# Two norm stages of a two-layer backbone: tokens turned by a diagonal matrix of inverse roots, modulation applied in the copies out of PSUM

## Chip, cores and metric

The program runs on one core of one Trainium2 chip, everything in float32. The metric is the device time of one launch in microseconds (us). Three runs of the kernel before gave 1813.14, 1815.0 and 1820.26 us, median 1815.0.

## What is computed

The reference has two layers over 256 latent and 256 context tokens of 1024 channels. Every layer starts with a modulated RMS norm of both streams, followed by a mixer whose first step is one large product:

```python
def rmsnorm(x, g):
    xf = x.astype(F32)
    y = xf * lax.rsqrt(jnp.mean(xf * xf, axis=-1, keepdims=True) + EPS)
    return (y * g.astype(F32)).astype(x.dtype)

def modulate(x, g, shift, scale):
    return rmsnorm(x, g) * (1.0 + scale) + shift

for layer in range(DEPTH):
    h_lat = modulate(x_lat, norm1_g[layer], mod_l[:, 0], mod_l[:, 1])
    h_ctx = modulate(x_ctx, norm1_g[layer], mod_c[0], mod_c[1])
    # layer 0: mixer_ab: h @ ab_w_in, latent attention, RG-LRU, output product
    # layer 1: mixer_cd: h @ cd_w_in, windowed attention, SSD, output product
    # then a second modulate and a mixture of experts on both streams (layer 1: latents only)
```

Shift and scale are rows of a product of the conditioning vector with `ada_w`; the kernel keeps them in a DRAM tensor `mod`, with (1 + scale) * g already folded together in the scale rows.

## The kernel before

The program is a chain of stages. Each stage is one `nc.Block()` with a program for each of the five engines (SyncE, ScalarE, VectorE, GpSimd, TensorE), and a block ends only when all five have finished theirs, so stages follow each other in time. Only DMAs that a stage issues without waiting for them reach over its end.

The tokens lie in SBUF as `x[128 tokens, 4 tiles, 1024]`; tiles 0 and 1 are the latent stream, 2 and 3 the context stream. The products that follow want the channels on the partitions: `ht[128, 8, 512]`, in which partition p of block k is channel 8p + k. `norm_stage` makes `ht` from `x`. It is called four times: for half 0 (ahead of the mixer) and half 1 (ahead of the experts) of both layers. It works in this order:

- SyncE (line 314) loads scale and shift rows of each stream, copied to all 128 partitions: 1 MB per stream. Behind them, by `prefetch` (line 358, `load_chunk`), it issues the first three chunks of the next product's weights into `ring[1]`: for layer 0 of 2, 1.5 and 2 MB, for layer 1 of 64 KB, 2 and 2 MB.
- ScalarE (line 321) squares the four tiles with a running sum per token; VectorE (334) makes means, ScalarE (323) roots, VectorE (336) reciprocals.
- VectorE, tile by tile: `h = x * root * scale` (line 340), then `h = h + shift` (line 342), 128x1024 each.
- TensorE (line 352): eight 128x128 transposes of each tile, against the identity, into two of the banks 0 to 3.
- ScalarE (line 328): two 128x512 copies of each tile from PSUM into `ht`.

After it comes `project_lru_stage` in layer 0 (products at line 541, the first 32 of them with 512 moving columns) and `project_ssd_stage` in layer 1 (line 1571; its first 32 products have only 16 moving columns, as they make the 16 step sizes of each token). The products of layer 0 start with chunk 0 of the weights, and take chunk 1 after four groups of eight.

Of the kernel before, what the change touches and what calls it, by code (L numbers as in the profile page):

```python
# [20 lines left out]
ALU = mybir.AluOpType  # L21
ACT = mybir.ActivationFunctionType
AX = mybir.AxisListType

P = 128
D = 1024
KC = D // P
SEQ = 256
NT = 4
LT = SEQ // P  # L30
T = NT * P
NMOD = 6
EPS = 1e-6
# [18 lines left out]
class Chain:  # L52
# [6 lines left out]
    def step(self, ins):  # L59
        self.n += 1  # L60
        ins.then_inc(self.sem, 1)
        self.engine.wait_ge(self.sem, self.n)
# [9 lines left out]
def cut(region, offset, *dims):  # L72

    n = int(np.prod(dims))
    flat = region[:, offset:offset + n]
    if len(dims) == 1:
        return flat
    names = "abcd"[:len(dims)]
    spec = f"p ({' '.join(names)}) -> p {' '.join(names)}"
    return flat.rearrange(spec, **{k: v for k, v in zip(names[1:], dims[1:])})  # L80
# [214 lines left out]
def mod_row(c, stream, layer, slot, n=1):  # L295

    at = (layer * NMOD + slot) * D
    return c.mod[stream, at:at + n * D].partition_broadcast(P)


def norm_stage(c, layer, half, tiles, prefetch=None, at=0):

    nc = c.nc
    streams = sorted({t // LT for t in tiles})
    gs = [cut(c.scr, at + s * 2 * D, 2, D) for s in range(2)]
    ss = c.stat[:, 0:NT]
    n = len(tiles)
    mod_in, sums, mean, root, h_ready, turned, ht_ready = (
        c.sem(x) for x in ("mod_in", "square_sums", "mean_ready", "root_ready", "h_ready", "h_turned", "ht_ready"))
    with nc.Block() as block:  # L310
        @block.sync
        def _(sp):
            for s in streams:
                sp.dma_start(gs[s].rearrange("p a b -> p (a b)"), mod_row(c, s, layer, 3 * half, 2)).then_inc(mod_in, 16)
            if prefetch:
                prefetch(sp)

        @block.scalar
        def _(act):
            for t in tiles:  # L320
                nc.scalar.activation(c.h[:, t, :], c.x[:, t, :], ACT.Square, accum_out=ss[:, t:t + 1]).then_inc(sums, 1)  # L321
            act.wait_ge(mean, 1)
            nc.scalar.activation(ss[:, 0:n], ss[:, 0:n], ACT.Sqrt).then_inc(root, 1)
            for t in tiles:
                act.wait_ge(turned, t + 1)
                for q in range(2):
                    b = 2 * (t % 2) + q
                    last = nc.scalar.activation(c.ht[:, 4 * q:4 * q + 4, t * P:(t + 1) * P], c.bank(b, 4, P), ACT.Copy)
                    last.then_inc(ht_ready, 1)

        @block.vector
        def _(dve):
            dve.wait_ge(sums, n)
            nc.vector.tensor_scalar(ss[:, 0:n], ss[:, 0:n], 1.0 / D, EPS, ALU.mult, ALU.add).then_inc(mean, 1)
            dve.wait_ge(root, 1)
            c.dve_chain.step(nc.vector.reciprocal(ss[:, 0:n], ss[:, 0:n]))
            dve.wait_ge(mod_in, 16 * len(streams))
            for t in tiles:
                g = gs[t // LT]
                c.dve_chain.step(nc.vector.scalar_tensor_tensor(c.h[:, t, :], c.x[:, t, :], ss[:, t:t + 1], g[:, 1, :],  # L340
                                                                ALU.mult, ALU.mult))
                nc.vector.tensor_tensor(c.h[:, t, :], c.h[:, t, :], g[:, 0, :], ALU.add).then_inc(h_ready, 1)  # L342

        @block.tensor
        def _(pe):
            for t in tiles:
                pe.wait_ge(h_ready, t + 1)
                if t >= 2:
                    pe.wait_ge(ht_ready, 2 * (t - 1))
                for k in range(KC):  # L350
                    b = 2 * (t % 2) + k // 4
                    last = nc.tensor.transpose(c.bank(b, 4, P)[:, k % 4, :], c.h[:, t, k::KC], c.ident[:])  # L352
                last.then_inc(turned, 1)


def load_chunk(c, sp, w_dram, w_in, chunk_of, ch):
# [869 lines left out]
def load_gate_up(c, m, sp, e, j):  # L1226
    load_matrix(c, m, sp, e, j, "moe_w_gate")
    load_matrix(c, m, sp, e, j, "moe_w_up")


def load_expert(c, m, sp, e, j):
    load_gate_up(c, m, sp, e, j)
    load_matrix(c, m, sp, e, j, "moe_w_down")


def load_router(c, m, sp):
    sp.dma_start(m.rw, c.i["router_w"].rearrange("(p k) e -> p k e", k=KC)).then_inc(m.small_in, 16)
    sp.dma_start(m.rb, c.i["router_b"].partition_broadcast(P)).then_inc(m.small_in, 16)
    sp.dma_start(m.count, c.i["count"]).then_inc(m.small_in, 16)
    sp.dma_start(m.before, c.i["before"].rearrange("p (a b) -> p a b", a=2)).then_inc(m.small_in, 16)  # L1240
# [189 lines left out]
def moe(c, m, tiles, out=None):  # L1430

    def ahead(sp):
        load_router(c, m, sp)
        load_expert(c, m, sp, 1, 1)

    norm_stage(c, m.layer, 1, tiles, ahead, at=15360 - 4 * D)
    route_stage(c, m, m.layer, tiles, lambda sp: load_gate_up(c, m, sp, 2, 2))
    experts_stage(c, m)
    combine_stage(c, m, m.layer, tiles, out)
# [406 lines left out]
def program(nc, ins, outs):  # L1846
    with ExitStack() as ctx:
# [14 lines left out]
        def first_chunks(sp):  # L1862
            for ch in range(3):
                load_chunk(c, sp, ins["ab_w_in"], w_in, CHUNKS_AB, ch)

        norm_stage(c, 0, 0, everyone, first_chunks)
        project_lru_stage(c, m, w_in)
        mla_stage(c, m, late)
# [5 lines left out]
        def clear_spare_blocks(pool):  # L1874
# [4 lines left out]
            for r in parts:  # L1879
# [6 lines left out]
                        QK ** -0.5, m.attn_t, m.p, m.pt, QK, sp_work=loads, md=last)  # L1886
        output_stage(c, 0, everyone, m.wo, (m.attn_t, m.gr), 11168, lambda sp: load_expert(c, mo, sp, 0, 0), clear_spare_blocks)
        moe(c, mo, everyone)
        c.clear_semaphores()

# [4 lines left out]
        def first_chunks(sp):  # L1895
            for ch in range(3):
                load_chunk(c, sp, ins["cd_w_in"], w_in, CHUNKS_CD, ch)

        norm_stage(c, 1, 0, everyone, first_chunks)
        project_ssd_stage(c, m, w_in)  # L1900
        wo_in = c.sem("cd_wo_in")

        def loads(sp):
# [8 lines left out]
                        HD ** -0.5, m.attn_t, m.p, m.pt, HD, sink=m.sink, mask=lambda t: (1 - t, m.far[:, t, :]))  # L1912
        output_stage(c, 1, range(LT), m.wo, (m.attn_t, m.y_t), 0)
        moe(c, mo, range(LT), outs["out"])


# [45 lines left out]
```

## Time and profile before

| | before |
|---|---|
| median of 3 runs | 1815.0 us |
| the profiled execution, its own time | 1814.77 us |
| its span, first to last instruction | 1813.0 us |
| mean granted TensorE clock | 0.851 |
| busy: TensorE, VectorE, ScalarE | 1316.5, 567.6, 395.9 us |
| norm stage of layer 0, half 0: first square to last copy | 40.34 to 60.12 us |
| norm stage of layer 1, half 0: first square to last copy | 986.90 to 1007.38 us |

Of the profile the reader needs three views. The timeline gives, for one engine, start, length and count of merged instructions, and in square brackets how long the engine was idle before them and who released it. The table of stretches gives busy time, granted TensorE clock (1.00 is 2.4 GHz, 0.50 is 1.2 GHz) and DMA share between two points of time. The view of one line gives the least, median and greatest duration of its instructions. PE is TensorE, DVE is VectorE, ACT is ScalarE, POOL is GpSimd, SP is SyncE.

### The profile page before, as it was taken

To read this page: it belongs to the slowest core of one execution; us is meant where nothing else is said; L and a number is where in the kernel's file an instruction comes from. 1 tells how busy PE (TensorE), PEld (TensorE's weight loads), DVE (VectorE), ACT (ScalarE), POOL (GpSimd) and SP (SyncE) were. 2 spreads that over 40 slices of the span, in tenths; PEclk is the share of its full clock that TensorE was granted. 3 is DMA by queue.
4 is the path that set the end of the run, shared out by engine and by line. 5 is a ranking of instruction groups with operands and counts; after the bars stand their busy time and mean duration, and the time that the engine had idled before them with its cause. 6 is when DMAs were issued, how large, how long until landed. Compare 5 with 4: busy or idle time off the path is not lost. (4 is left out here: it accounts for less than half of the span.)

```text
span 1813.0 us, 35116 instructions
## 1 busy us (share of the span) xinstructions
PE 1316.5 (73%) x14404; PEld 774.9 (43%) x14405; DVE 567.6 (31%) x1511; ACT 395.9 (22%) x867; POOL 39.3 (2%) x81
## 2 busy tenths in 40 slices
PE   3897979895767897667990998949766555576572
PEld 2455646544433454333660646725343222243241
DVE  0537555413311222111224435567231000011012
ACT  1243224202111232111221222235112111122120
POOL 0002010100000000000001000000000000000000
PEclk8898999995888899788995798959978777798796
DMA  7422987256699999999925310050289999999995
GB/s 267 155 76 79 330 294 287 90 210 285 252 430 428 429 429 429 429 429 429 429 103 194 136 66 4 1 232 1 88 368 430 430 428 429 430 428 428 429 429 221
DMA packets 82533, 519.35 MB, mean 286 GB/s; under 512 B 12045, under 2 KB 16370, under 8 KB 57002
## 3 DMA queue, kind: packets, MB, share of 16 engines
q1 hardware_dynamic: 73632, 494.03, 66.2%
q10 hardware_dynamic: 5146, 13.78, 2.0%
q0 software_dynamic: 3696, 10.73, 1.6%
q8 instruction: 40, 0.66, 0.1%
q14 instruction: 19, 0.16, 0.0%
HBM read 501.50 MB, written 17.01 MB: 286 GB/s over the span
## 5 line engine op out<-in xcount | busy, mean ns | idle before, releaser
L1305 PE MATMUL bank<-sb_ring,sb_scratch 128*32 128x256 f32 x3968 | 275.4, 439 | 149.7 <-DMA sb_ring<-in_moe_w_up 136.5
L1305 PEld LDWEIGHTS bank<-sb_ring,sb_scratch 128*32 128x32 f32 x3968 | 144.9, 126 | 277.4 <-issue 220.2
L1384 DVE TENSOR_TENSOR sb_scratch<-sb_scratch,bank 128x128 f32<-128x128 f32 x88 | 25.3, 287 | 742.1 <-ACT sb_scratch L1337 742.1
L1305 PE MATMUL bank<-sb_scratch 128*32 128x256 f32 x1664 | 125.6, 468 | 95.1 <-DMA sb_scratch<-in_moe_w_up 92.7
L1341 ACT ACTIVATE sb_ht<-bank 32x256 f32<-32x256 f32 x352 | 132.3, 376 | 274.8 <-PE bank L1315 271.8
L1293 PE MATMUL bank<-sb_h,sb_scratch 128*32 128x256 f32 x2256 | 140.7, 384 | 13.8 <-DVE sb_scratch L1371 13.8
L1305 PEld LDWEIGHTS bank<-sb_scratch 128*32 128x32 f32 x1664 | 63.3, 134 | 156.3 <-issue 137.0
L1315 PE MATMUL bank<-sb_ring,sb_scratch 128*32 128x256 f32 x1984 | 119.2, 380 | 9.8 <-issue 9.4
L1337 ACT ACTIVATE sb_scratch<-bank 128x128 f32<-128x128 f32 x88 | 24.4, 278 | 464.2 <-PE bank L1305 464.1
L1293 PEld LDWEIGHTS bank<-sb_h,sb_scratch 128*32 128x32 f32 x2256 | 74.1, 111 | 63.0 <-DVE sb_scratch L1371 14.1
L1315 PEld LDWEIGHTS bank<-sb_ring,sb_scratch 128*32 128x32 f32 x1984 | 67.5, 110 | 54.8 <-issue 20.5
L352 PE MATMUL bank<-sb_ident,sb_h 128*128 128x128 f32 x112 | 25.7, 402 | 82.7 <-DVE sb_h L342 82.7
L1571 PE MATMUL bank<-sb_ring,sb_ht 128*128 128x16 f32 (+2 forms) x192 | 60.7, 474 | 5.8 <-DVEq L1734 4.4
L352 PEld LDWEIGHTS bank<-sb_ident,sb_h 128*128 128x128 f32 x112 | 20.6, 215 | 88.7 <-DVE sb_h L342 88.7
L541 PE MATMUL bank<-sb_ht,sb_ring 128*128 128x512 f32 x128 | 57.0, 607 | 1.4 <-PEq L310 1.4
L1571 PE MATMUL bank<-sb_ht,sb_ring 128*128 128x512 f32 x128 | 57.2, 607 | 0.0
L1315 PE MATMUL bank<-sb_scratch 128*32 128x256 f32 x832 | 49.9, 380 | 4.1 <-issue 3.8
L1376 DVE STREAM_TRANSPOSE sb_scratch<-bank 128x256 f32<-128x256 f32 x90 | 38.9, 432 | 38.6 <-PE bank L1293 38.6
L1571 PEld LDWEIGHTS bank<-sb_ring,sb_ht 128*128 128x128 f32 x192 | 38.8, 242 | 24.4 <-issue 17.5
L321 ACT ACTIVATE sb_h<-sb_x 128x1024 f32<-128x1024 f32 x14 | 14.6, 1044 | 158.3 <-PEq L1024 89.8
L195 PE MATMUL bank<-sb_ring 128*32 128x128 f32 x1280 | 39.1, 277 | 8.2 <-DMA sb_ring<-in_ada_w 8.2
L1044 PE MATMUL bank<-sb_ring,sb_scratch 128*128 128x512 f32 x96 | 43.2, 592 | 0.0
(299 smaller groups left out, 1550.5 us busy)
## 6 DMA issues: line engine op xcount, KB each, us to landing
sb_ring<-in_moe_w_gate SPq DMA_DIRECT2D x44, 2048.0 KB, 28.4
sb_ring<-in_moe_w_up SPq DMA_DIRECT2D x44, 2048.0 KB, 32.9
sb_ring<-in_moe_w_down SPq DMA_DIRECT2D x44, 2048.0 KB, 35.5
sb_ring<-in_ada_w SPq DMA_DIRECT2D x20, 2048.0 KB, 14.5
sb_scratch<-in_moe_w_gate SPq DMA_DIRECT2D x20, 2048.0 KB, 32.9
sb_scratch<-in_moe_w_up SPq DMA_DIRECT2D x20, 2048.0 KB, 37.6
sb_scratch<-in_moe_w_down SPq DMA_DIRECT2D x20, 2048.0 KB, 39.9
sorted_out<-sb_ht ACTq DMA_DIRECT2D x88, 128.0 KB, 6.0
```

The lines of the kernel that those rows point to most:

```text
L195: last = self.c.nc.tensor.matmul(self.c.ps[bank][32 * q:32 * q + 32, 0:P], self.condk[:, k, :], w[:, k, q * P:(q + 1) * P], start=k == 0, ...
L352: last = nc.tensor.transpose(c.bank(b, 4, P)[:, k % 4, :], c.h[:, t, k::KC], c.ident[:])
L541: last = nc.tensor.matmul(c.ps[u % NB][:, 0:rhs.shape[1]], lhs, rhs, start=k == 0, stop=k == KC - 1)
L1044: last = nc.tensor.matmul(c.ps[u % 4][:], src, wo[:, k, q * BANK:(q + 1) * BANK], start=k == 0, stop=k == KC - 1)
L1293: last = nc.tensor.matmul(c.ps[0][MB * q:MB * q + MB, 0:DQ], m.pick[:, t, :], c.h[:, t, q * DQ:(q + 1) * DQ], start=t == 0, stop=t == nt - 1)
L1305: last = nc.tensor.matmul(c.bank(1, 2, FQ)[MB * q:MB * q + MB, :, :], m.xt[:, k, :], m.gu[j][:, :, k, q * FQ:(q + 1) * FQ], start=k == 0, ...
L1315: last = nc.tensor.matmul(c.ps[3][MB * q:MB * q + MB, 0:DQ], m.hmt[:, k, :], m.down[j][:, k, q * DQ:(q + 1) * DQ], start=k == 0, stop=k == ...
L1337: nc.scalar.activation(m.sg, c.ps[1][:, 0:FQ], ACT.Silu).then_inc(silu_r, 1)
L1341: last = nc.scalar.activation(m.yb[j][:, q * DQ:(q + 1) * DQ], c.ps[3][MB * q:MB * q + MB, 0:DQ], ACT.Copy)
L1376: v.transpose(m.xt, c.bank(0, MB, KC).rearrange("p j k -> p k j")).then_inc(xt_ready, 1)
L1384: v.tensor_tensor(m.hm, m.sg, c.ps[1][:, FQ:2 * FQ], ALU.mult).then_inc(hm_ready, 1)
L1571: last = nc.tensor.matmul(c.ps[bank_of(u)][:, 0:rhs.shape[1]], lhs, rhs, start=k == 0, stop=k == KC - 1)
```

## The change

`norm_stage` as it was is now called `norm_rows_stage` and still serves half 1 of both layers. Half 0 of both layers (ahead of the mixers) gets a new `norm_stage`:

- The 2 MB of broadcast rows are replaced by two loads of shift and scale as columns (`modcol`, each partition its own 8 shifts and 8 scales: two pieces of 32 bytes per partition and stream).
- The squares carry the factor 1/1024 themselves, and epsilon is the bias of the root. Means, roots and reciprocals are made per stream, so those of the latents don't wait for the context tiles.
- VectorE multiplies the identity by the tile's inverse roots: a 128x128 diagonal matrix (`diag`) for each tile.
- TensorE multiplies `x` with that diagonal, by `matmul` rather than `transpose`: eight 128x128 products a tile, into banks 4 to 7, two tiles of one stream side by side. The result is turned and normed at once.
- The copies out of PSUM, 128x256 each, apply scale and shift, which are now numbers per partition: banks 4 and 6 by ScalarE, 5 and 7 by VectorE.

```diff
-def norm_stage(c, layer, half, tiles, prefetch=None, at=0):
+def norm_rows_stage(c, layer, half, tiles, prefetch=None, at=0):
...
+def norm_stage(c, layer, half, tiles, prefetch=None, at=0):
...
+        @block.sync
+            for s in streams:
+                sp.dma_start(modcol[:, s], c.mod[s, row:row + 2 * D].rearrange("(a p k) -> p a k", a=2, k=KC)).then_inc(cols_in, 16)
...
+        @block.scalar
+            for s in streams:
+                for t in range(s * LT, (s + 1) * LT):
+                    nc.scalar.activation(c.h[:, t, :], c.x[:, t, :], ACT.Square, scale=D ** -0.5, accum_out=ss[:, t:t + 1]).then_inc(means, 1)
...
+                nc.scalar.activation(of_stream, of_stream, ACT.Sqrt, bias=eps).then_inc(roots, 1)
+            act.wait_ge(cols_in, 16 * len(streams))
+            for s in streams:
+                for b in (0, 2):
+                    act.wait_ge(turned, 4 * s + b + 1)
+                    for k in (2 * b, 2 * b + 1):
+                        last = nc.scalar.activation(c.ht[:, k, s * W:(s + 1) * W], c.bank(4 + b, 2, W)[:, k % 2, :], ACT.Identity,
+                                                    bias=modcol[:, s, 0, k:k + 1], scale=modcol[:, s, 1, k:k + 1])
...
+        @block.vector
+            for s in streams:
+                dve.wait_ge(roots, s + 1)
+                step(v.reciprocal(of_stream, of_stream))
+                for t in range(s * LT, (s + 1) * LT):
+                    v.tensor_scalar(diag[:, t, :], c.ident[:], ss[:, t:t + 1], None, ALU.mult).then_inc(scaled, 1)
+            dve.wait_ge(cols_in, 16 * len(streams))
+            for s in streams:
+                for b in (1, 3):
+                    dve.wait_ge(turned, 4 * s + b + 1)
+                    for k in (2 * b, 2 * b + 1):
+                        last = v.tensor_scalar(c.ht[:, k, s * W:(s + 1) * W], c.bank(4 + b, 2, W)[:, k % 2, :],
+                                               modcol[:, s, 1, k:k + 1], modcol[:, s, 0, k:k + 1], ALU.mult, ALU.add)
...
+        @block.tensor
+            for s in streams:
+                for b in range(4):
+                    if s > 0:
+                        pe.wait_ge((act_evicted, dve_evicted)[b % 2], 2 * (s - 1) + b // 2 + 1)
+                    for t in range(s * LT, (s + 1) * LT):
+                        pe.wait_ge(scaled, t + 1)
+                        for k in (2 * b, 2 * b + 1):
+                            last = nc.tensor.matmul(c.bank(4 + b, 2, LT, P)[:, k % 2, t % LT, :], c.x[:, t, k::KC], diag[:, t, :],
+                                                    start=True, stop=True)
+                    last.then_inc(turned, 1)
...
-    norm_stage(c, m.layer, 1, tiles, ahead, at=15360 - 4 * D)
+    norm_rows_stage(c, m.layer, 1, tiles, ahead, at=15360 - 4 * D)
```

What VectorE has in a row in layer 0 between the barrier at the start of the norm stage and its end, before (a name in square brackets is the semaphore waited for; `mod_in` is the broadcast rows, `dve_chain` VectorE's own last result):

```order
L334 TENSOR_SCALAR sb_stat<-sb_stat 128x4 [waits square_sums_29]
L336 RECIPROCAL sb_stat<-sb_stat 128x4 [waits root_ready_31]
L340 SCALAR_TENSOR_TENSOR sb_h<-sb_x,sb_stat,sb_scratch 128x1024 [waits mod_in_28,dve_chain_2]
L342 TENSOR_TENSOR sb_h<-sb_h,sb_scratch 128x1024 [waits dve_chain_2]
L340 SCALAR_TENSOR_TENSOR sb_h<-sb_x,sb_stat,sb_scratch 128x1024
L342 TENSOR_TENSOR sb_h<-sb_h,sb_scratch 128x1024 [waits dve_chain_2]
```

And with the change (`x_turned` is TensorE's finished bank):

```order
L403 RECIPROCAL sb_stat<-sb_stat 128x2 [waits roots_ready_31]
L405 TENSOR_SCALAR sb_scratch<-sb_ident,sb_stat 128x128 [waits dve_chain_2]
L405 TENSOR_SCALAR sb_scratch<-sb_ident,sb_stat 128x128
L403 RECIPROCAL sb_stat<-sb_stat 128x2 [waits roots_ready_31]
L405 TENSOR_SCALAR sb_scratch<-sb_ident,sb_stat 128x128 [waits dve_chain_2]
L405 TENSOR_SCALAR sb_scratch<-sb_ident,sb_stat 128x128
L411 TENSOR_SCALAR sb_ht<-bank,sb_scratch 128x256 [waits x_turned_33,mod_columns_in_28]
L411 TENSOR_SCALAR sb_ht<-bank,sb_scratch 128x256
```

The eight passes over 1024 columns are gone; four 128x128 passes and eight 128x256 copies stand in their place, and both reciprocals and all four diagonals come ahead of the first copy.

ScalarE in the same place, with the change:

```order
L381 ACTIVATE sb_h,sb_stat<-sb_x 128x1024 x2
L386 ACT_TABLE_LOAD [waits square_means_30]
L386 ACTIVATE sb_stat<-sb_stat 128x2 [waits eps_set_29]
L381 ACTIVATE sb_h,sb_stat<-sb_x 128x1024 x2
L386 ACTIVATE sb_stat<-sb_stat 128x2 [waits square_means_30]
L392 ACTIVATE sb_ht<-bank,sb_scratch 128x256 [waits x_turned_33,mod_columns_in_28]
L392 ACTIVATE sb_ht<-bank,sb_scratch 128x256
```

The root of the first stream has moved ahead of the last two squares, and there is one table load, as before.

TensorE in the same place, before and then with the change:

```order
L352 MATMUL bank<-sb_ident,sb_h 128x128 [waits h_ready_32]
L352 MATMUL bank<-sb_ident,sb_h 128x128 x7
L352 MATMUL bank<-sb_ident,sb_h 128x128 [waits ht_ready_34,h_ready_32]
L310 UNCONDITIONAL_BRANCH
L541 MATMUL bank<-sb_ht,sb_ring 128x512 [waits ab_w_in0_25]
```

```order
L424 MATMUL bank<-sb_scratch,sb_x 128x128 [waits roots_spread_32]
L424 MATMUL bank<-sb_scratch,sb_x 128x128
L424 MATMUL bank<-sb_scratch,sb_x 128x128 [waits roots_spread_32,ht_even_34]
L424 MATMUL bank<-sb_scratch,sb_x 128x128 [waits roots_spread_32,ht_odd_35]
L368 UNCONDITIONAL_BRANCH
L614 MATMUL bank<-sb_ht,sb_ring 128x512 [waits ab_w_in0_25]
```

There are 32 instructions before and 32 after, but they wait for a diagonal in place of a finished tile of `h`, and in the second stream for the bank to be copied out.

## Rows read from the trace of the kernel before

**Rows 1.** Timeline of layer 0's norm stage, ScalarE (start us, length us, instruction, [idle before])

```profile
40.34 1.06 ACT L321 ACTIVATE sb_h<-sb_x 128x1024 f32<-128x1024 f32 x1 [37.29 <-PEq L244]
42.35 0.19 ACT L321 ACTIVATION_READ_ACCUMULATOR sb_h<-sb_x 128x1 f32 x1
...
44.63 1.28 ACT L323 ACT_TABLE_LOAD   x1
45.92 0.21 ACT L323 ACTIVATE sb_stat<-sb_stat 128x4 f32<-128x4 f32 x1
...
59.03 1.09 ACT L328 ACTIVATE sb_ht<-bank 128x512 f32<-128x512 f32 x2 [0.59 <-PE bank L352]
```

**Rows 2.** The same stage, VectorE

```profile
46.16 0.18 DVE L336 RECIPROCAL sb_stat<-sb_stat 128x4 f32<-128x4 f32 x1 [1.35 <-ACT sb_stat L323]
47.88 1.28 DVE L340 SCALAR_TENSOR_TENSOR sb_h<-sb_x,sb_stat,sb_scratch 128x1024 f32<-128x1024 f32 x1 [1.54 <-DMA sb_scratch<-mod]
49.20 1.22 DVE L342 TENSOR_TENSOR sb_h<-sb_h,sb_scratch 128x1024 f32<-128x1024 f32 x1
```

**Rows 3.** The same stage and the start of the next, TensorE

```profile
50.48 1.97 PE L352 MATMUL bank<-sb_ident,sb_h 128*128 128x128 f32 x8 [13.21 <-DVE sb_h L342]
...
57.84 1.16 PE L352 MATMUL bank<-sb_ident,sb_h 128*128 128x128 f32 x8 [0.52 <-DVE sb_h L342]
```

**Rows 4.** Timeline of layer 1's norm stage: ScalarE's first and last, TensorE's first and next stage

```profile
986.90 1.06 ACT L321 ACTIVATE sb_h<-sb_x 128x1024 f32<-128x1024 f32 x1 [31.18 <-PEq L124]
1006.29 1.09 ACT L328 ACTIVATE sb_ht<-bank 128x512 f32<-128x512 f32 x2 [1.31 <-PE bank L352]
...
996.98 1.97 PE L352 MATMUL bank<-sb_ident,sb_h 128*128 128x128 f32 x8 [42.93 <-DVE sb_h L342]
1007.68 12.18 PE L1571 MATMUL bank<-sb_ring,sb_ht 128*128 128x16 f32 x64 [1.43 <-PEq L310]
```

**Rows 5.** Stretches, TensorE: length, busy (count), granted clock, DMA share, GB/s

```profile
57.00:57.50 0.50, 0.32 (x2) 0.84 1.03 381
60.50:61.00 0.50, 0.50 (x1) 0.57 1.04 381
63.50:64.00 0.50, 0.50 (x2) 0.52 0.55 125
64.00:64.50 0.50, 0.50 (x3) 1.00 0.27 63
1006.00:1007.00 1.00, 0.25 (x2) 0.97 0.00 0
1009.00:1010.00 1.00, 1.00 (x9) 0.74 0.11 12
1023.00:1024.00 1.00, 1.00 (x3) 0.94 1.04 408
```

**Rows 6.** Attention of layer 0, full clock, TensorE: transposes (L921) and plain products (L909)

```profile
L921 PE MATMUL bank<-sb_ident,sb_scratch x96: 270/273/331, 270.5 to 352.5; 128*128 128x128 f32 x96
L909 PE MATMUL bank<-sb_h,sb_ring x192: 272/273/323, 272.7 to 353.7; 128*64 128x128 f32 x192
278.10 1.09 PE L909 MATMUL bank<-sb_h,sb_ring 128*64 128x128 f32 x8
```

**Rows 7.** Layer 1 after the norm, VectorE: copies of two neighbouring groups of 16-column products

```profile
1016.49 0.17 DVE L1703 COPY sb_scratch<-bank 128x16 f32<-128x16 f32 x1 [3.24 <-PE bank L1571]
1019.90 0.17 DVE L1703 COPY sb_scratch<-bank 128x16 f32<-128x16 f32 x1 [3.24 <-PE bank L1571]
```

**Rows 8.** Views of single lines: duration ns, least/median/greatest

```profile
L1749 DVE TENSOR_SCALAR sb_ring<-bank,sb_scratch x44: 472/473/484, 1106.7 to 1179.4; 128x256 f32<-128x256 f32 x44
L785 ACT ACTIVATE sb_ring<-bank x8: 384/384/386, 219.0 to 243.4; 128x256 f32<-128x256 f32 x8
L1424 DVE TENSOR_SCALAR sb_scratch<-sb_scratch,sb_wsel x6: 745/746/931, 967.0 to 1805.3; 128x1024 f32<-128x1024 f32 x6
```

**Rows 9.** DMA issues and landings: chunks of ab_w_in (L358), then small loads (L515)

```profile
L358 SPq DMA_DIRECT2D sb_ring<-in_ab_w_in x3: 567/2969/4942, 41.2 to 44.8; - x3
DMA to landing us min/median/max: 12.0/15.6/17.9
...
L515 SPq DMA_DIRECT2D sb_scratch<-in_lru_w_a x4: 610/616/638, 62.2 to 65.5; - x4
DMA to landing us min/median/max: 2.2/2.3/2.4
```

More of the change, by code:

```diff
@@ L353, in _ @@
                 last.then_inc(turned, 1)
+def norm_stage(c, layer, half, tiles, prefetch=None, at=0):
+    nc = c.nc
+    streams = sorted({t // LT for t in tiles})
+    W = LT * P
+    ss, eps = c.stat[:, 0:NT], c.stat[:, NT:NT + 1]
+    diag = cut(c.scr, at, NT, P)
+    modcol = cut(c.scr, at + NT * P, 2, 2, KC)
+    cols_in, eps_set, means, roots, scaled, turned, act_evicted, dve_evicted = (
+        c.sem(x) for x in ("mod_columns_in", "eps_set", "square_means", "roots_ready", "roots_spread", "x_turned", "ht_even", "ht_odd"))
+    with nc.Block() as block:
+        @block.sync
+        def _(sp):
+            row = (layer * NMOD + 3 * half) * D
+            for s in streams:
+                sp.dma_start(modcol[:, s], c.mod[s, row:row + 2 * D].rearrange("(a p k) -> p a k", a=2, k=KC)).then_inc(cols_in, 16)
+            if prefetch:
+                prefetch(sp)
+        @block.scalar
+        def _(act):
+            for s in streams:
+                for t in range(s * LT, (s + 1) * LT):
+                    nc.scalar.activation(c.h[:, t, :], c.x[:, t, :], ACT.Square, scale=D ** -0.5, accum_out=ss[:, t:t + 1]).then_inc(means, 1)
+                if s == 0:
+                    act.wait_ge(eps_set, 1)
+                act.wait_ge(means, (s + 1) * LT)
+                of_stream = ss[:, s * LT:(s + 1) * LT]
+                nc.scalar.activation(of_stream, of_stream, ACT.Sqrt, bias=eps).then_inc(roots, 1)
[6 more added lines that the diff above has]
+                                                    bias=modcol[:, s, 0, k:k + 1], scale=modcol[:, s, 1, k:k + 1])
+                    last.then_inc(act_evicted, 1)
+        @block.vector
+        def _(dve):
+            step, v = c.dve_chain.step, nc.vector
+            v.memset(eps, EPS).then_inc(eps_set, 1)
+            for s in streams:
+                of_stream = ss[:, s * LT:(s + 1) * LT]
+                dve.wait_ge(roots, s + 1)
[9 more added lines that the diff above has]
+                                               modcol[:, s, 1, k:k + 1], modcol[:, s, 0, k:k + 1], ALU.mult, ALU.add)
+                    last.then_inc(dve_evicted, 1)
+        @block.tensor
+        def _(pe):
+            for s in streams:
[8 more added lines that the diff above has]
+                    last.then_inc(turned, 1)
```

## The prediction, on record before the changed kernel was run

> **What bounds the kernel now.** I read the timelines of the two norm stages first, then the table of stretches for TensorE's clock, then the views of single lines for prices. Stages follow each other behind barriers, so what counts is each changed stage's time from its first square to its last copy, and what the next stage finds when it starts.
>
> In layer 0 that time runs from 40.34 to 59.03 + 1.09 = 60.12, 19.8 us [rows 1]; in layer 1 from 986.90 to 1006.29 + 1.09 = 1007.38, 20.5 us [rows 4]. The end is set by a line of waits: four squares (4.3 us), table load and root (to 46.13), reciprocal, a wait of 1.54 us for the broadcast rows, and then four tiles of 1.28 + 1.22 us of VectorE [rows 1, 2]. TensorE starts only at 50.48, 10.1 us into the stage, and sits idle 0.5 us before every later tile, waiting for `h` [rows 3]. So VectorE bounds the stage, with the rows' landing ahead of it; TensorE's transposes are hidden but for the last tile.
>
> **The change, step by step, times from the stage's start.**
>
> *Up to the first product.* Two squares end at 42.35 + 0.19 = 42.54, that is 2.2 us; table load 1.28 and root 0.21 bring 3.7; reciprocal 0.18, 3.95 [rows 1, 2]. A 128x128 diagonal is not in the trace: 128x1024 of the same operation takes 0.75 [rows 8], a reciprocal of 4 columns 0.18, so it lies between 0.18 and 0.75; I take 0.2, nearest the small end. TensorE starts at **4.2** where it started at 10.1.
>
> *The products.* This is the term that grows. A transpose leaves one record in the trace, a plain float32 product two: attention has 96 products to be turned, and L921 has 96 records, while the products with the turned blocks are also 96 and L909 has 192 [rows 6]. So the 32 products make 64 records. One record with its weights costs at half clock 3.41 us / 16 = 0.213 [rows 7]; at full clock (1.09 - 0.27) / 7 = 0.117 [rows 6]. A product is then 0.43 or 0.23 us. I take 0.22 for the latter, since moving 128 columns at 2.4 GHz should take no more than half of 0.43.
>
> The clock decides the sum. The transposes began at 50.48 and the clock rose at about 57.1, 6.6 us later, with TensorE idle in between; the dense 512-column products began at 60.43 and the clock, which fell at 60.57, was back at 64.0, 3.5 us later [rows 3, 5]. The new products follow each other without a gap, so I take a rise 5 us after their start, with bounds of 3.4 and 6.7. Five us at half clock are 5 / 0.43 = 11.7 products; the other 20.3 take 4.5; together **9.5** (bounds 8.7 and 10.3).
>
> Nothing else is behind this. Stream 1's roots: squares to about 6.0, root, reciprocal and diagonals to 6.9, while TensorE is busy with stream 0 until past 10. A bank of four products takes 0.9 us or more; its two copies take 0.77 on ScalarE (384 each) and 0.95 on VectorE (473 each) [rows 8], and the engines alternate, so each has two banks' time for one. The columns: two small loads at the head of the queue. Small loads of 256 pieces landed in 2.3 us [rows 9]; first needed at 4.2 + 1.7 = 5.9. VectorE's copies stand behind both diagonals of stream 1, at 6.9, when its first bank is done at 7.6.
>
> *The tail.* Last product's length beyond the spacing and the semaphore 0.2, VectorE's last two copies 0.95. The stage takes 4.2 + 9.5 + 0.2 + 0.95 = **14.85 us**. Saved: 19.8 - 14.85 = **4.9** in layer 0, 20.5 - 14.85 = **5.6** in layer 1.
>
> *The next stage's weights.* The first chunk of layer 0 landed 12.0 after its issue at 41.2, so at 53.2 [rows 9], behind 2 MB of rows that are no longer loaded; the new stage ends at 40.34 + 14.85 = 55.2. It is there even unmoved. The second is needed four groups (over 27 us) later. In layer 1 the first chunk has 64 KB. No wait takes the place.
>
> *The clock in the next stage.* Before, the clock was high for only 3.4 us around the last transposes and fell just as layer 0's dense products started: 3.4 us at half clock, 1.7 lost [rows 5]. Now TensorE has been dense at full clock for over 4 us, and the pause is 0.95 + 0.2 + 0.3 (barrier) = 1.5 us, so I expect it to stay high: **1.7** saved. That stage ends on products and a VectorE chain that waits for them, so it passes on. In layer 1 the clock fell at 1009.5 in the 16-column products and stayed low until 1023 [rows 5]; it will fall there again, perhaps a little later: **0.4**.
>
> *Removed at no gain:* the 1.54 us wait for rows is within the 10.1 already counted; half 1's stages are unchanged.
>
> Sum: 4.9 + 5.6 + 1.7 + 0.4 = 12.6. The profiled execution took 1814.77 us, 0.2 under the median of 1815.0, so **1802.2 us**. With rises at 3.4 us: 5.7 + 6.4 + 1.7 + 1.5 = 15.3, 1799.5; at 6.7 us and no warm start: 4.1 + 4.8 = 8.9, 1805.9.
>
> **A rule beside the row.** The count of records says that a float32 product costs two transposes (0.43 against 0.21 us at half clock). The Trainium skill, page "TensorE: Matmul & The Clock Gate", section "Terms", says that transpose mode is four times faster for float32. By that rule a product would be 0.85 and 0.44 us, 5.9 products in the first 5 us and 26.1 x 0.44 = 11.5 after: 16.5 in place of 9.5, 7 us more in each stage, and a kernel of 1816. No row here shows a factor of four; this is rival D.
>
> **Rivals.**
>
> *B. The clock never rises inside the stage.* Then 32 x 0.43 = 13.7, the stage takes 19.0, and only 0.8 + 1.5 = 2.3 us are saved: **1812.5**, no change. For it: in layer 1 the clock stayed low from 996.98 to 1006 under transposes, 9 us [rows 4, 5]. Against: those had gaps, and gapless 512-column products raised it in 3.5 us.
>
> *C. The columns land late: the slower side.* The two loads are of 32-byte pieces, 512 in all, read from `mod`, ahead of 5.5 MB in one queue. After the banks of stream 0 are full (at about 10) TensorE stops. If the columns land at L, two copies (0.9), sixteen products at half clock (6.8) and the tail (1.15) follow: the stage takes L + 8.9, and breaks even at L = 11. At L = 17.9, as the last chunk [rows 9], it takes 26.8: 7.0 + 6.3 us lost, **1828**. Against: the 2.3 us of 256 pieces [rows 9]; each piece would have to cost many times as much.
>
> *D. A float32 product costs four transposes:* about **1816**, as worked out.
>
> *E. The saved time is partly given back* in the next stages: a fall of the clock in the 1.5 us pause, its return later than before, and banks waited for. About half of the gain: **1807.5**. For it: the clock fell at 60.57 after a stretch with a pause of the same length [rows 5]. Against: in that stretch TensorE was idle for well over half.
>
> **How the numbers follow.** The forecast has 0.78, B 0.08, C 0.03, D 0.03, E 0.08. The likeliest case's own range is 1799.5 to 1806. To leave out at most 2 in 10 I add E and a margin for sizes I took from other operations (diagonal, copies with two operands): **1798 to 1809**. A measurement of this kernel tells 0.5%, 9.1 us, from no change: the line is at 1805.9. Faster: nearly all of the forecast and a little of E, **0.79**. Same: B, most of E and D, **0.17**. Slower: C and a part of D, **0.04**.
>
> **What would show it.** In the new profile: the first product 4.2 us after the first square; 64 records at L424 in each stage, none with an idle time before it that matters; the clock rising once in the stage, 3.4 to 6.7 us after the first product; the last copy 14 to 15.7 us after the first square, by VectorE (L411); the first product at L614 at full clock. The forecast is wrong if TensorE waits for a copy or for the columns, if there are more than two records per product, or if the clock stays at 0.50 to the stage's end.

## The result: slightly slower, and the profile after

The changed kernel takes 1820.84 us (median of 22 runs, 1812.95 to 1828.7), the kernel before 1814.93 us in 22 runs beside it (1810.04 to 1822.27). The ratio is 1.0033, 95% interval 1.0022 to 1.0044: some 6 us slower, a small loss but clear of the noise, where 12.6 us faster was forecast. The profiled execution of the changed kernel took 1821.84 us, its span is 1820.0 us, the mean granted clock 0.850 as before (0.851).

Timeline of layer 0's norm stage in the changed kernel, ScalarE, VectorE and TensorE, against [rows 1 to 3]; lines of the new `norm_stage` are 358 to 426, and L614 is the first product of the next stage:

```profile
40.34 1.06 ACT L381 ACTIVATE sb_h<-sb_x 128x1024 f32<-128x1024 f32 x1 [37.23 <-PEq L244]
42.61 1.28 ACT L386 ACT_TABLE_LOAD   x1
58.44 1.02 ACT L392 ACTIVATE sb_ht<-bank,sb_scratch 128x256 f32<-128x256 f32 x2 [2.79 <-PE bank L424]
...
44.44 0.48 DVE L405 TENSOR_SCALAR sb_scratch<-sb_ident,sb_stat 128x128 f32<-128x128 f32 x2
60.35 0.99 DVE L411 TENSOR_SCALAR sb_ht<-bank,sb_scratch 128x256 f32<-128x256 f32 x2 [2.82 <-PE bank L424]
...
44.78 15.53 PE L424 MATMUL bank<-sb_scratch,sb_x 128*128 128x128 f32 x64 [7.55 <-DVE sb_scratch L405]
61.66 8.82 PE L614 MATMUL bank<-sb_ht,sb_ring 128*128 128x512 f32 x20 [1.35 <-PEq L368]
```

TensorE starts 4.4 us into the stage, near the forecast (4.2; it was 10.1 before), has 64 records, as forecast, and no idle time. But the 64 take 15.5 us, not 9.5. ScalarE and VectorE wait for TensorE's banks, up to 2.8 us each time. The stage ends at 61.34, 21.0 us after its start, against 19.8 before. Layer 1's is as long, where it had 20.5 before, against [rows 4]:

```profile
991.03 1.06 ACT L381 ACTIVATE sb_h<-sb_x 128x1024 f32<-128x1024 f32 x1 [31.17 <-PEq L124]
...
1011.04 0.99 DVE L411 TENSOR_SCALAR sb_ht<-bank,sb_scratch 128x256 f32<-128x256 f32 x2 [2.82 <-PE bank L424]
...
995.46 15.54 PE L424 MATMUL bank<-sb_scratch,sb_x 128*128 128x128 f32 x64 [37.27 <-DVE sb_scratch L405]
```

The clock did rise. The table of stretches for TensorE in layer 0's stage of the changed kernel (length, busy, count, granted clock, DMA share, GB/s; a count takes in what overlaps an edge):

```profile
45.00:49.00 4.00, 4.00 (x17) 0.50 1.05 396
51.00:55.00 4.00, 4.00 (x19) 1.00 1.06 380
```

Twice the clock, and almost the same number of records in four microseconds, 17 and 19. They are 0.240 us apart at 1.2 GHz and 0.238 at 2.4 GHz. So I looked at the loading of the stationary operand, which comes ahead of each record and is listed as PEld. The views of the two lines, changed kernel (both layers) and then the transposes of the kernel before in the stretch at full clock (57.8 to 59), against [rows 6]:

```profile
L424 PEld LDWEIGHTS bank<-sb_scratch,sb_x x128: 312/336/341, 44.8 to 1010.5; 128*128 128x128 f32 x128
```

```profile
L352 PEld LDWEIGHTS bank<-sb_ident,sb_h x8: 185/193/208, 57.8 to 58.6; 128*128 128x128 f32 x8
```

A load of `x[:, t, k::KC]` for a plain product takes 338 ns at half and 336 at full clock; the load of `h[:, t, k::KC]`, with the same step of eight elements, for a transpose takes 226 ns at half and 193 at full clock. The theory after this reading: the step in the stationary operand sets the pace of plain float32 products. The rival: a plain product with 128 moving columns costs 0.24 us a record in any layout. The second question is where the rest of the 6 us comes from, since the two stages, up to the next one's start, grew by only 1.2 and, over three executions of each kernel, 1.0 us on the mean.

### The profile page after: what moved, and what is told of

Same layout as the page of the kernel before. It is cut to its first block and busy times, and to the rows that moved or that the text cites. A ratio compares the mean times of both kernels' runs of the same rounds, so it can differ in the third digit from the quotient of the medians.

```text
span 1820.0 us, 35264 instructions
## 1 busy us (share of the span) xinstructions
PE 1335.8 (73%) x14468; PEld 798.6 (44%) x14469; DVE 558.2 (31%) x1521; ACT 395.6 (22%) x869; POOL 39.1 (2%) x81
## 5 line engine op out<-in xcount | busy, mean ns | idle before, releaser
L1366 PEld LDWEIGHTS bank<-sb_h,sb_scratch 128*32 128x32 f32 x2256 | 74.4, 111 | 62.7 <-DVE sb_scratch L1444 14.1
L1388 PEld LDWEIGHTS bank<-sb_ring,sb_scratch 128*32 128x32 f32 x1984 | 67.6, 110 | 54.7 <-issue 20.5
L424 PE MATMUL bank<-sb_scratch,sb_x 128*128 128x128 f32 x128 | 31.1, 416 | 44.8 <-DVE sb_scratch L405 44.8
L614 PE MATMUL bank<-sb_ht,sb_ring 128*128 128x512 f32 x128 | 55.3, 593 | 1.4 <-PEq L368 1.4
L424 PEld LDWEIGHTS bank<-sb_scratch,sb_x 128*128 128x128 f32 x128 | 30.7, 336 | 45.4 <-DVE sb_scratch L405 45.4
L195 PEld LDWEIGHTS bank<-sb_ring 128*32 128x32 f32 x1280 | 34.9, 112 | 14.5 <-DMA sb_ring<-in_ada_w 8.7
## 6 DMA issues: line engine op xcount, KB each, us to landing
sb_ring<-in_moe_w_down SPq DMA_DIRECT2D x44, 2048.0 KB, 35.9
sb_scratch<-in_moe_w_up SPq DMA_DIRECT2D x20, 2048.0 KB, 37.8
```

What stands on the lines that cost most here:

```text
L195: last = self.c.nc.tensor.matmul(self.c.ps[bank][32 * q:32 * q + 32, 0:P], self.condk[:, k, :], w[:, k, q * P:(q + 1) * P], start=k == 0, ...
L424: last = nc.tensor.matmul(c.bank(4 + b, 2, LT, P)[:, k % 2, t % LT, :], c.x[:, t, k::KC], diag[:, t, :], start=True, stop=True)
L614: last = nc.tensor.matmul(c.ps[u % NB][:, 0:rhs.shape[1]], lhs, rhs, start=k == 0, stop=k == KC - 1)
L1366: last = nc.tensor.matmul(c.ps[0][MB * q:MB * q + MB, 0:DQ], m.pick[:, t, :], c.h[:, t, q * DQ:(q + 1) * DQ], start=t == 0, stop=t == nt - 1)
L1388: last = nc.tensor.matmul(c.ps[3][MB * q:MB * q + MB, 0:DQ], m.hmt[:, k, :], m.down[j][:, k, q * DQ:(q + 1) * DQ], start=k == 0, stop=k == ...
```

## The experiments

**Layout (blocks_diag).** Channels in blocks of 128, so the stationary operand is contiguous; the weights' rows follow, and shift and scale come as rows that TensorE turns. Three of the edited places (`...` stands for lines left out):

```diff
-                            last = nc.tensor.matmul(c.bank(4 + b, 2, LT, P)[:, k % 2, t % LT, :], c.x[:, t, k::KC], diag[:, t, :],
+                            last = nc.tensor.matmul(c.bank(4 + b, 2, LT, P)[:, k % 2, t % LT, :], c.x[:, t, k * P:(k + 1) * P], diag[:, t, :],
...
-                 w_dram.rearrange("o (p k) n -> p (o k) n", k=KC)[:, :, c0:c0 + n]).then_inc(w_in[ch % 3], 16)
+                 w_dram.rearrange("o (k p) n -> p (o k) n", k=KC)[:, :, c0:c0 + n]).then_inc(w_in[ch % 3], 16)
...
-                sp.dma_start(modcol[:, s], c.mod[s, row:row + 2 * D].rearrange("(a p k) -> p a k", a=2, k=KC)).then_inc(cols_in, 16)
+                sp.dma_start(modrow[16 * s:16 * s + 16, :], c.mod[s, row:row + 2 * D].rearrange("(r p) -> r p", p=P)).then_inc(cols_in, 16)
...
+            nc.tensor.transpose(c.ps[0][:, 0:32], modrow, c.ident[0:32, 0:32]).then_inc(cols_t, 1)
```

> Channels kept in blocks of 128 (block k of ht is channels 128k to 128k+127, and the weights are loaded to match), so that the stationary operand of the diagonal products is contiguous, not every eighth element; shift and scale come as 32 rows of 128 and are turned by one small transpose. All else as in the change. Theory stride (the products are spaced by the loading of a stationary operand with a step of 32 bytes): records go from 0.24 us apart to 0.213 at half and about 0.11 at full clock, the 64 take 9 to 10 us in place of 15.5, each norm stage 14.5 to 15.5 us, and the kernel is some 12 us faster than the change, near 1808. Rival (a plain float32 product with 128 moving columns costs 0.24 us a record whatever the layout): 15.5 us as now, no change of time.

Measured: 1803.43 us (6 runs), kernel before 1817.49 in 11 runs on the same chip, ratio 0.9919 (0.9904 to 0.9934). Its timeline and the load's view in layer 0:

```profile
44.84 8.79 PE L430 MATMUL bank<-sb_scratch,sb_x 128*128 128x128 f32 x64 [2.13 <-DVE sb_scratch L409]
54.99 15.26 PE L620 MATMUL bank<-sb_ht,sb_ring 128*128 128x512 f32 x35 [1.35 <-PEq L370]
```

```profile
L430 PEld LDWEIGHTS bank<-sb_scratch,sb_x x64: 192/192/338, 44.8 to 53.2; 128*128 128x128 f32 x64
```

The same 64 records take 8.8 us. At full clock the load takes 192 ns and the records are 0.112 us apart (0.238 in the changed kernel); at half clock they are 0.213 apart (0.240). The stage, from its first instruction to the next stage's, takes 14.5 us in both layers; to the last copy in layer 0 it is 14.25, where the prediction had 14.85. The rival falls. The kernel gained 14.1 us on the kernel before, more than the 12.6 that the prediction had for the change, and came out lower than the 1808 expected of this run.

**How large a step (step_2, step_4).** As blocks_diag, with the channels in blocks of 256 or 512 that are read with a step of 2 or 4 elements:

```diff
-                            last = nc.tensor.matmul(c.bank(4 + b, 2, LT, P)[:, k % 2, t % LT, :], c.x[:, t, k * P:(k + 1) * P], diag[:, t, :],
+                            last = nc.tensor.matmul(c.bank(4 + b, 2, LT, P)[:, k % 2, t % LT, :], c.x[:, t, k // 2 * 256 + k % 2:(k // 2 + 1) * 256:2], diag[:, t, :],
```

> The diagonal products with a step of 2 elements (8 bytes) in the stationary operand (channels in blocks of 256, each read in two interleaved halves, weights and shift and scale to match). Contiguous gave 64 records in 8.8 us, a step of 8 gave 15.5. Theory rate (an element costs by the bytes that its step passes over): a small step costs nothing, 8.8 us. Theory packing (only contiguous elements are read two at a time or more): any step costs the same as 8, 15.5 us.

> The same with a step of 4 elements (16 bytes). Theory rate: between, or still 8.8 us. Theory packing: 15.5 us.

Measured, layer 0, step 2 and then step 4 (timeline, a stretch at full clock, the load's view):

```profile
44.79 10.57 PE L432 MATMUL bank<-sb_scratch,sb_x 128*128 128x128 f32 x64 [2.27 <-DVE sb_scratch L409]
...
51.00:55.00 4.00, 4.00 (x36) 1.00 1.06 386
...
L432 PEld LDWEIGHTS bank<-sb_scratch,sb_x x64: 196/197/331, 44.8 to 55.0; 128*128 128x128 f32 x64
```

```profile
43.26 15.20 PE L432 MATMUL bank<-sb_scratch,sb_x 128*128 128x128 f32 x64 [1.94 <-DVE sb_scratch L409]
...
50.00:54.00 4.00, 4.00 (x19) 1.00 1.06 383
...
L432 PEld LDWEIGHTS bank<-sb_scratch,sb_x x64: 309/329/332, 43.3 to 57.9; 128*128 128x128 f32 x64
```

In layer 1 they took 9.76 and 15.20 us. The 10.6 and 9.8 us of step 2 are more than the 8.8 of the contiguous layout, but most of that is the clock: in layer 0 it rose 6.2 us after the first product, in blocks_diag 2.9. At the same clock the records lie so (distance of one record from the next, us):

| step in elements (bytes) | at half clock | at full clock | load at full clock, ns |
|---|---|---|---|
| 1 (4), blocks_diag | 0.213 | 0.112 | 192 |
| 2 (8), step_2 | 0.213 | 0.118 | 197 |
| 4 (16), step_4 | 0.233 | 0.233 | 329 |
| 8 (32), changed kernel | 0.240 | 0.238 | 336 |

A step of 8 bytes costs next to nothing, 16 bytes cost nearly all that 32 do. Neither theory had that shape: it is a jump between 8 and 16 bytes, not a slope, and not any step at all. At half clock the step costs little, since the contiguous records are 0.213 us apart there too; what it takes away is the gain of the full clock. The totals of these single runs were 1811.6 and 1818.59 us, with 1816.43 for one run of the kernel before on the same chip.

**Transposes in place of products (scaled_turn).** VectorE multiplies by the inverse root, TensorE transposes as before, the rest as in the change:

```diff
-                    v.tensor_scalar(diag[:, t, :], c.ident[:], ss[:, t:t + 1], None, ALU.mult).then_inc(scaled, 1)
+                    v.tensor_scalar(c.h[:, t, :], c.x[:, t, :], ss[:, t:t + 1], None, ALU.mult).then_inc(scaled, 1)
...
-                            last = nc.tensor.matmul(c.bank(4 + b, 2, LT, P)[:, k % 2, t % LT, :], c.x[:, t, k::KC], diag[:, t, :],
-                                                    start=True, stop=True)
+                            last = nc.tensor.transpose(c.bank(4 + b, 2, LT, P)[:, k % 2, t % LT, :], c.h[:, t, k::KC], c.ident[:])
```

> VectorE multiplies x by the inverse root (one pass of 128x1024 a tile, 0.75 us) into h, and TensorE transposes h as before the change, one record a block; copies with scale and shift per partition as in the change. If the transposes with the same step cost 0.213 us at half clock and 0.11 to 0.13 at full (as the old ones did) the products' 15.5 us become 6 to 7, each norm stage 12 to 13.5 us in place of 21.0, the kernel 14 to 17 us faster than the change and 8 to 11 faster than before, near 1805. If the step costs a transpose as much as a product in this arrangement, 32 records at 0.24 take 7.7 us and the stage 14.

Measured: 1800.85 us (6 runs, 1792.93 to 1801.87), ratio to the kernel before 0.9893 (0.9872 to 0.9914). The timeline of layer 0, then of layer 1:

```profile
45.41 6.40 PE L424 MATMUL bank<-sb_ident,sb_h 128*128 128x128 f32 x32 [7.98 <-DVE sb_h L405]
...
986.04 5.59 PE L424 MATMUL bank<-sb_ident,sb_h 128*128 128x128 f32 x32 [37.77 <-DVE sb_h L405]
```

Stages of 12.6 and 11.8 us against 20.0 and 20.7. Its median is the lowest of all here, below both kernels; it is 2.6 us under blocks_diag, whose 6 runs (1802.13 to 1807.84) don't overlap with it. It keeps what was good in the change (roots per stream, scale and shift in the copies, no broadcast rows) and leaves out the diagonal. The expected total was 1805, and 12 to 13.5 us were expected for each stage.

**Which layer costs the time (layer0_only, layer1_only).** The new stage in one layer, `norm_rows_stage` in the other:

```diff
-        norm_stage(c, 1, 0, everyone, first_chunks)
+        norm_rows_stage(c, 1, 0, everyone, first_chunks)
```

> The change in layer 0's norm stage alone; layer 1's is as before. Theory direct (the time is lost in the changed stage and the one after it): stage +1.2 us, next stage -1.7 to 0, so -0.5 to +1.2 us against before. Theory knock-on (what the change does to the time at which later stages begin, against the changes of the clock, costs more than the stages themselves): layer 0's attention takes 91.8 or more in place of 89.9, and the kernel is 2 to 4 us slower than before.

> The change in layer 1's norm stage alone. Theory direct: norm stage and the product stage behind it together +1.2 us, so +1.2 us. Theory knock-on: attention of layer 1 takes 56.5 in place of 54.4 besides, so +3 us, and layer 0's attention is as before at 89.9.

Measured, 12 runs each, with 23 of the kernel before on the same chip (median 1818.12): layer 0 alone 1816.76, ratio 0.9990 (0.9977 to 1.0003); layer 1 alone 1822.95, ratio 1.0020 (0.9999 to 1.0042). In layer 0 the gain of the warm start (106.4 us in place of 108.1 in the stage behind) pays for the longer stage, as theory direct had it for the total; knock-on's 2 to 4 us did not come, though layer 0's attention was 92.9 us in the profile. In layer 1 the median is 4.8 us up, more than stage and next stage account for. The interval touches no change, so this alone would not carry the point. And in the profile of layer1_only neither theory had the stages right: layer 0's attention took 92.4 us where 89.9 was expected, and layer 1's 58.6, where knock-on had 56.5.

**Profiles repeated (before_again, before_third, after_again, after_third).** Nothing is edited in these.

> A second profile of the kernel before, to see which stages differ from one execution to the next with nothing changed. Theory S (the extra time sits in fixed places that the change moved): every stage but the mixers' clock-dependent ones repeats within 0.3 us, and attention of layer 0 again takes near 89.9 us and its output stage 57.1. Theory N (noise of the clock, the extra 6 us is not from the change in this one execution): attention and output stages scatter by 2 to 4 us between executions of the same kernel, by how long the clock is at 0.50 in them.

> A second profile of the changed kernel. Both theories: 64 records at L424 in 15.5 us in each norm stage, stages of 21.0 us, since the records were 0.24 us apart at either clock. Theory S: attention of layer 0 and its output stage again near 93.7 and 59.3 us. Theory N: they scatter, and may be as short as before.

> A third profile of the kernel before. Theory systematic (the change in layer 1 costs some 4 us from that norm stage to the end of the attention): that stretch takes 286.6 to 290 us, as in the four profiles so far with the old stage in layer 1 (mean 287.8 without the pause). Theory chance: it is spread as with the new stage, 290 to 294.6.

> A third profile of the changed kernel. Theory systematic: the stretch takes 290 us or more (four profiles so far: 289.9 to 294.6, mean 291.8), attention 56.5 or more. Theory chance: it may be 286.6.

The kernel before repeated itself, as theory S had it; the changed kernel's attention and output product of layer 0 did not. From the norm stage of layer 1 to the end of its attention the stretch was 286.6 to 286.7 us in all three of one and 289.9 to 290.0 in all three of the other, as theory systematic had it; but it was also 290.0 in layer0_only, which has the old stage in layer 1. Lengths in us, each from the first instruction of a stage to the first of the next, read from the timelines; three executions of each kernel:

| stage | before | changed |
|---|---|---|
| layer 0 norm | 20.0, 20.2, 19.9 | 21.3, 21.3, 21.3 |
| layer 0 products after it | 108.1, 108.1, 108.1 | 106.4, 108.0, 106.4 |
| next (latent attention's inputs) | 96.2, 96.0, 96.3 | 94.6, 96.5, 95.5 |
| layer 0 attention | 89.9, 89.9, 90.0 | 93.7, 91.8, 90.7 |
| layer 0 output product | 57.1, 57.1, 57.1 | 59.3, 57.1, 58.8 |
| layer 1 norm | 20.7, 19.4, 20.8 | 21.3, 21.3, 21.3 |
| layer 1 products and SSD | 188.9, 190.5, 188.9 | 189.6, 189.7, 189.7 |
| layer 1 attention | 54.5, 54.5, 54.5 | 56.5, 56.5, 56.5 |
| span | 1813.0, 1812.7, 1812.2 | 1820.0, 1815.1, 1815.8 |

By the means, the norm stages add 1.2 and 1.0, the products after them take 1.2 off and add 0.3: +1.3 together. Attention adds 2.2 and 2.0 and the first output product 1.3, though none of their instructions is changed: +5.5. The other stages give 2.4 back, which leaves the 4.4 us between the mean spans. So most of the loss in these six executions lies in stages that the change doesn't touch.

That the change causes it is not shown by this, least of all in layer 0. layer1_only and pause_before (below) run the kernel before's own instructions up to layer 1, and in both layer 0's attention took 92.4 us and the output product 58.8, as long as in the changed kernel. Of the 14 executions that were profiled only the three of the kernel before had 89.9 to 90.0 in this attention; the others had 90.7 to 93.7. The start of the attention, of the kernel before and then of layer1_only:

```profile
264.64:268.80 4.16, 4.12 (x6) 0.59 0.65 217
```

```profile
262.66:273.40 10.74, 8.99 (x24) 0.68 0.60 199
```

TensorE was at half clock for 3.4 us of this attention before, and for 10.1 us in layer1_only: 6.9 at its start and the rest at its end.

Layer 1's attention shows what such a difference is made of. The stretches, TensorE, of the kernel before from the stage's start at 1218.99, and then of the changed kernel from its start at 1224.4:

```profile
1218.99:1231.00 12.01, 11.03 (x23) 0.50 0.35 149
1231.00:1236.00 5.00, 4.65 (x23) 0.97 0.00 0
```

```profile
1224.40:1236.40 12.00, 11.01 (x23) 0.50 0.33 139
1236.40:1241.40 5.00, 5.00 (x16) 0.50 0.01 2
1241.40:1245.00 3.60, 3.35 (x18) 0.99 0.00 0
```

Both start at half clock, on the same work. Before, the full clock is back after 12 us; in the changed kernel after 17, and the stage is 2.0 us longer. In layer1_only it took 22 us and the stage 58.6. Its stretches:

```profile
1236.00:1241.00 5.00, 5.00 (x16) 0.50 0.00 0
1241.00:1246.00 5.00, 5.00 (x17) 0.50 0.01 2
1246.00:1250.00 4.00, 3.89 (x18) 0.99 0.00 0
```

In the 5 us before the clock came back TensorE was busy throughout in each of the three, and in layer1_only for 10 us ahead of these as well. So the busy time of these stretches doesn't say why it came back when it did; the guess was that it has to do with when the stage begins.

**A pause ahead of attention (pause_before, pause_after).** To move that beginning, one idle copy on ScalarE at the end of the stage ahead:

```diff
                 act.sem_inc(copied, 1)
+            c.act_chain.step(nc.scalar.activation(c.scr[:, 3200:4500], c.scr[:, 3200:4500], ACT.Copy))
```

> The kernel before with one idle copy on ScalarE (about 1.3 us) at the end of the stage ahead of layer 1's attention, so that attention begins that much later against the clock's changes. Theory knock-on: attention takes 56.5 in place of 54.4 though none of its work is changed, so the kernel gains 3.3 us and not 1.3. Rival (attention's length has to do with what the change left in memory or in PSUM, not with when it starts): 54.4.

> The changed kernel with the same idle copy. Theory knock-on: attention of layer 1, 56.5 in both profiles of the changed kernel, now takes 54.4; the pause is paid back. Rival: 56.5.

Measured: theory knock-on missed both. pause_before took 54.5 us in attention and pause_after 56.6, which is what the rival had (totals of single runs 1819.89 and 1828.37). As a test it was weak: the stages ahead came out at other lengths in these two executions (SSD 190.2 and 192.2), so the pause, 1.5 us, did not move the beginning to where it was meant. What can be read from all 14 executions is the time from the clock's last fall before attention, inside the SSD stage, to attention's start, and how long the clock then stayed at half, from that fall to its return within attention:

| from fall to start, us | half clock, from fall to return, us | layer 1 attention, us | executions |
|---|---|---|---|
| 35.4, 35.5, 35.5, 35.7 | 47.8 | 54.5, 54.5, 54.5, 54.4 | before, before_again, before_third, scaled_turn |
| 35.9, 36.0 | 58.0 | 58.6, 58.6 | step_2, layer1_only |
| 36.3 | 54.6 | 56.7 | blocks_diag |
| 37.4, 37.5, 37.5, 37.5, 37.5 | 54.6 | 56.6, 56.5, 56.5, 56.5, 56.7 | pause_after, changed, after_again, after_third, layer0_only |
| 37.8, 39.0 | 51.2 | 54.8, 54.5 | step_4, pause_before |

The code of layer 1's norm stage does not decide the length: scaled_turn and step_4 have a new stage there and 54.4 and 54.8, layer0_only has the old one and 56.7. That also speaks against the rival, what the change left in memory. The executions fall into groups by the moment of the start, but not in a simple order: a start 0.2 us later (35.7, 35.9) went with 4.2 us more, one 0.3 us later (37.5, 37.8) with 1.7 us less. No run set the moment on purpose and hit it, so it is not shown as a cause; nor is it shown that the change moves it for the worse in most executions.

## Why the prediction was wrong, step by step

- **Start at 4.2 us:** right (4.4). A diagonal took 0.28 us against 0.2 assumed, the root with a bias 0.30 against 0.21. Nothing waited for the columns: their two loads landed in 1.7 to 1.9 us. Rival C is out.
- **64 records:** right: two for each plain float32 product.
- **What a record costs: the step that failed.** The prediction took 0.213 us a record at half clock and 0.11 at full, from products whose stationary operand is contiguous [rows 6, 7], and gave the stationary operand `x[:, t, k::KC]` with its step of eight elements no cost of its own. That the transposes read with the same step and were fast said nothing of plain products. The changed kernel's 64 records took 15.5 us and not 9.5, 0.24 each at both clocks. The full clock is where it went: the forecast had 20.3 products at 0.22 us there, at 0.476 they take 5.2 us more (an estimate from the 0.238 us between records). The rest of the term was sound: with the step taken out it measured 8.8, with the clock rising 2.9 us after the first product, which is earlier than the forecast's bound of 3.4 (step_2, with the rise at 6.2, took 10.6). Twice 6 us of the forecast gain were lost here.
- **Clock inside the stage:** rose 5.5 us after the first product in layer 0 and 3.7 in layer 1, forecast 5, and bought nothing, since the load did not get faster with it. Rival B had 13.7 us for the products, nearer than 9.5, and its total of 1812.5, but its condition, a clock that stays low, did not come. By rival D, the factor of four from the Trainium skill, page "TensorE: Matmul & The Clock Gate", section "Terms", 16.5 us were due. The measured 15.5 is near. A factor of about four is seen at full clock with the step of eight (0.476 us a product, 0.11 a transpose in scaled_turn), but not at half clock (0.48 against 0.213), and contiguous it is two: two records 0.112 us apart against one for a transpose. So the factor is not the cause.
- **The tail and the copies:** two copies 0.99 us on VectorE (0.95 forecast); ScalarE's with scale and bias 560 ns each, not the 384 of a plain copy [rows 8]. No copy held TensorE up.
- **Warm start of the next stage, 1.7 us:** right in layer 0: 106.4 against 108.1 in two of three executions. TensorE's pause between the stages was 1.35 us, and in these two the clock stayed at 2.4 GHz over it. In after_again it fell in that pause, at 59.7, and was back at 63.2: there the stage took 108.0, as rival E had it. Layer 1's 0.4 did not come: 189.7 against a mean of 189.4 before.
- **What had no term at all:** attention and output product, together 5.5 us in the profiled executions. The prediction carried saved time through unchanged stages as if their lengths were fixed, and they differ by up to 4 us between executions. Rival E had the clock in the next stages, but only as giving back a gain. (Half of the gain of 12.6 from 1814.8 is 1808.5, and not its 1807.5; nothing hangs on it.)

With the record at its true cost, the prediction's own sum would have been: stage 4.4 + 15.5 + 0.2 + 0.99 = 21.1, so 1.3 and 0.6 us lost, 1.7 won in layer 0: no change. The medians of 22 runs are 6 us apart. In the profiled executions what lies above the sum is in attention and output product, less 2.4 us that other stages gave back; whether the change causes it, and how, is open.

## What to carry to other kernels

Before a transpose is replaced by a float32 product that does arithmetic on the way, look at the step of its stationary operand: contiguous or 8 bytes apart a record took 0.11 to 0.12 us at full clock, 16 or 32 bytes apart 0.23 to 0.24 us, at either clock, and there are two for each product. Scaling ahead of a transpose cost one short VectorE pass (0.75 us for 128x1024) and was the faster way here. And stages that nobody edited came out 2 to 4 us longer or shorter, also with the same instructions ahead of them: compare several profiled executions stage by stage before a few tenths of a per cent are put down to the edited lines.

## What was not expected of the hardware

- Loading 128x128 float32 for a plain product: 192 ns contiguous, 197 with a step of 2 elements, 329 with 4, 336 with 8, at full clock; at half clock 329 to 338 in every layout. For a transpose with a step of 8: 193 ns at full clock. Why the transpose is spared is open.
- Records 0.24 us apart at both granted clocks, 0.50 and 1.00: a rise of the clock that changes nothing.
- An unchanged attention stage of 54.4 to 54.8, 56.5 to 56.7 or 58.6 us, by whether the clock came back 12 to 13, 17 to 18 or 22 us after its start, and the same value to 0.1 us in three executions of one kernel. In all 14 executions the stretch at half clock that ends there had one of four lengths: 47.8, 51.2, 54.6 or 58.0 us. Whether the moment of the stage's start decides this is open.
